# The output projection moved into the block of the mixers: last chunk's tail between dense products, samples' columns later

## The chip, the cores and the metric

One core of a Trainium2 chip. The metric is the device time of one execution in microseconds (us), smallest is best. The engines are TensorE (PE; PEld is its weight load), VectorE (DVE), ScalarE (ACT), GpSimd (POOL) and SyncE (SP, which issues most DMAs). They run side by side, each in its own program order, and wait for each other on semaphores.

## The reference, cut to what matters

One step of a hybrid decoder layer, for a prompt of 1024 tokens and 8 samples of 4 tokens (32 sample tokens; 1056 in all). Everything is float32.

```python
u = rmsnorm(x); q, k, v, z, xbc, dt = split(u @ w_in)
A = dilated_attention(q, k, v)              # prompt; samples attend to a cache of keys and values
y, ssm_state = ssd(conv(xbc), dt)           # Mamba-2 scan, chunks of 128 tokens
B = grouped_rmsnorm((y + d_skip * x) * silu(z))
h = x + concat(A, B) @ w_out                # the output projection: the stage of this change
y = h + relu(rmsnorm(h) @ w_up) ** 2 @ w_down
```

## The kernel before, in words

Features lie on the 128 partitions, tokens along the free axis. A dense product in float32 is three products of fp32r values: each operand is split into a high part (a cast) and a low part (the value minus the high part), and high by high, high by low and low by high are summed in PSUM. The 1056 token columns of a product are three groups of 352 columns (`GROUPS`, NG = 3), so one output tile costs, for each of KD = 8 input tiles, nine matmuls of 352 columns. The third group ends with the 32 sample columns.

The program has stages. `project` makes q, k, v. `weave` (in a block of its own, which stays open) makes the prompt's attention between the dense products of the remaining projections. `mixers` (line 1338) goes into the same block: eight rounds n = 0 to 7, each with chunk n of the prompt's scan and sample n's attention over the cache. `outward` (line 1987) holds the output projection, the samples' scan, and the feed-forward part. Before, `program.close()` in `build` (line 2661) ends the block between `mixers` and `outward`, and `outward` opens its own (line 2079).

**Start of the mixers.** SP loads the samples' q, keys, bias, then the rows of cumulated decays `ssd_m` (`load_rows(0)`, line 1421, 1 MB, behind a wait at line 1451 for a matmul twelve ticks before the end of `weave`), the chunk (`load_chunk`), the cache's values. GpSimd clears the diagonal query tile `sa_qdiag`, waits for the end of `weave`, clears the state, places sample 0's query (`place`, lines 1668 to 1678), clears two small tiles, prepares the samples' bias, and multiplies x by dt (`weigh_x`). TensorE does the scores of sample 0 (line 1497, behind `placed`), then turns x (`turn_x`, line 1552), `chunk_start`, and begins round 0 with `off(0, 0)` (line 1580). ScalarE makes the decays from the loaded rows (`segment`, lines 1753 and 1756) and then copies the turned x (`keep_x`, line 1764). VectorE starts with a wait for the stores of z (line 1935).

**Tail of the mixers.** After the last value products (lines 1520, 1524), TensorE turns y twice (`turn_y`, line 1560), gathers the sample's output (`sample_gather`, line 1542: 16 matmuls) and sums squares (`norm_sums`, line 1569). Between them VectorE has `keep_own` (1927), `keep_norm` of round 6 (1886, 1889), `add_skip` twice (1857), `gate` (1864), `keep_out` (1932), `keep_norm` of round 7; ScalarE `square` (1805); GpSimd `skipped` (1739) and `sum_squares` (1699, 1701).

**Start of outward.** The first half of w_out (tiles o = 0 to 7, which multiply A) is done in steps q = 8 o + k: `step(q)` (lines 2184 to 2201) is the nine matmuls of input tile k for output tile o, into the PSUM tile `wo_psa`. Input tile k of A comes from memory into one of three slots of `stage` (`load_a`), ScalarE casts it (`cast_a`, 2357), VectorE subtracts (`split_a`, 2445). Slots 0 to 2 and the first two weight tiles are loaded ahead, during round 5 (`ahead.load`, line 1479). A slot is loaded again after its `split_a`. The samples' scan stands in front of step 0 (transposes 2231 to 2236, sums 2241, decays 2244), behind step 3 (`ss_in`, 2253) and then between steps: `carried(b)` at the steps in OFF_AT, the first at q = 7, and `grown(b)` at those in STATE_AT. VectorE makes the masks for sample b in `own_rows(b)`. GpSimd splits the weights (2094, 2096): tile u needs slot u % 2 free (`w_used`).

```python
pe.wait_ge(w_split, o + 1); pe.wait_ge(a_lo_made, k + 1)     # step, o == 0
OFF_AT = {q: i // 2 for i, q in enumerate(PIECES) if i % 2 == 0}
for sem in retired: pool.sem_clear(sem)                       # outward's POOL, at u == 2
```

`kit.clear` and the loop at u == 2 set the semaphores of a finished stage back; `kit.prime` raises those of the feed-forward loops.

## Time and profile before

| | |
|---|---|
| time, median of 3 runs | 2105.92 us (2097.87 to 2106.04) |
| the profiled execution's own time | 2102.71 us |
| its span, first to last instruction | 2100.9 us |
| TensorE | busy 1996.1 us, 95% of the span |
| VectorE, ScalarE, GpSimd | busy 49%, 33%, 45% |
| mean granted TensorE clock | 0.987 of full speed |

The span starts at 0. The mixers take about 845 to 1101 us, outward begins at 1103.7 us. A line of a timeline gives start, length, engine, source line, operation, output and inputs, count, and in brackets how long the engine had been idle and what ended that. TensorE has two clock levels, 1.2 and 2.4 GHz; PEclk gives the granted one as a share of the higher, so 0.50 is the lower level and 1.00 the higher.

### The profile page before, as it was taken

Reading aid. Unit: us, or ns where it says so; the run is one execution under the profiler, and the core shown is the slowest. Engines: PE = TensorE matmul, PEld = TensorE weight load, DVE = VectorE, ACT = ScalarE, POOL = GpSimd, SP = SyncE. Lnnn points to the kernel's source line nnn. Section 1 sums busy time; section 2 is a strip of 40 time slices with the busy share of each in tenths; the row PEclk is TensorE's granted clock in tenths of the full one; section 3 lists DMA queues with packets and bytes.
Section 4 is the critical chain, followed back from the end, with each engine's and each line's share of the span. In section 5 each row is a group of like instructions: output and inputs, shape, how many; then the busy total and the mean of one; then the engine's idle time right before and its main releaser. Section 6 shows DMA issues by size and latency. Waiting matters only on the chain. (4 is left out here: it accounts for less than half of the span.)

```text
span 2100.9 us, 30132 instructions
## 1 busy us (share of the span) xinstructions
PE 1996.1 (95%) x11992; PEld 1816.7 (86%) x11992; DVE 1030.3 (49%) x1355; ACT 699.8 (33%) x1194; POOL 944.6 (45%) x580
## 2 busy tenths in 40 slices
PE   8999999888888999899989999999999999999999
PEld 7999998777777888565557789999999999999998
DVE  5888803877767665577767552522222212121212
ACT  5344323666666775555532021210010101010010
POOL 4688614777657665334423123243333334232332
PEclk9999999999999999899998999999999999999999
DMA  4354436444443443687845433111111111111112
GB/s 167 143 192 162 148 114 128 114 115 107 96 102 97 118 129 117 238 271 258 260 156 198 172 106 123 41 51 41 51 40 50 40 50 40 50 40 50 40 50 93
DMA packets 117926, 239.36 MB, mean 114 GB/s; under 512 B 29996, under 2 KB 63660, under 8 KB 116285
## 3 DMA queue, kind: packets, MB, share of 16 engines
q1 hardware_dynamic: 94956, 205.69, 31.2%
q10 hardware_dynamic: 22864, 32.25, 4.7%
q8 instruction: 69, 1.13, 0.2%
q14 instruction: 37, 0.30, 0.1%
HBM read 187.78 MB, written 58.67 MB: 117 GB/s over the span
## 5 line engine op out<-in xcount | busy, mean ns | idle before, releaser
L913 POOL TENSOR_SCALAR att_p<-att_p,att_rden 128x128 f32<-128x128 f32 (+7 forms) x128 | 250.6, 1965 | 132.9 <-DVE att_rden L1053 132.9
L2104 POOL CAST wo_hi<-wo_raw 128x1024 fp32r<-128x1024 f32 x64 | 66.7, 1042 | 492.6 <-issue 240.5
L2428 ACT ACTIVATE r_sq<-stage 128x1056 f32<-128x1056 f32 x32 | 34.8, 1088 | 624.5 <-DVE stage L2617 624.5
L2106 POOL TENSOR_TENSOR wo_lo<-wo_raw,wo_hi 128x1024 fp32r<-128x1024 f32 x64 | 187.3, 2926 | 5.1
L1058 DVE TENSOR_TENSOR att_pTlo<-att_t_ps,att_pThi 128x512 fp32r<-128x512 f32 x192 | 106.2, 553 | 109.0 <-ACT att_pThi L1173 107.6
L1173 ACT ACTIVATE att_pThi<-att_t_ps 128x512 fp32r<-128x512 f32 x192 | 93.3, 486 | 124.4 <-PE att_t_ps L995 117.3
L966 PE MATMUL dense_ps<-u_hi,w_hi 128*128 128x352 f32 x480 | 115.5, 342 | 16.3 <-DVE conv_pre L1085 7.8
L673 DVE RECIPROCAL proj_rinv<-proj_rinv 128x1056 f32<-128x1056 f32 x16 | 108.0, 6753 | 9.8 <-ACT proj_rinv L563 9.8
L2627 DVE TENSOR_TENSOR h<-h,wo_psa 128x1056 f32<-128x1056 f32 x32 | 40.2, 1255 | 144.2 <-PE wo_psa L2344 144.2
L1165 ACT ACTIVATE att_p<-att_p,att_min 128x128 f32<-128x128 f32 (+7 forms) x128 | 98.7, 772 | 32.7 <-DVE att_min L1071 31.7
L966 PE MATMUL dense_ps<-u_hi,w_lo 128*128 128x352 f32 x480 | 108.2, 334 | 0.0
L966 PE MATMUL dense_ps<-u_lo,w_hi 128*128 128x352 f32 x480 | 108.1, 333 | 0.0
L966 PEld LDWEIGHTS dense_ps<-u_hi,w_hi 128*128 128x128 f32 x480 | 81.3, 191 | 26.2 <-issue 17.4
L995 PE MATMUL att_t_ps<-const,att_p 128*128 128x128 f32 x576 | 95.6, 275 | 5.9 <-DVE att_pTlo L1058 2.0
L2627 DVE TENSOR_TENSOR h<-h,wo_psb 128x1056 f32<-128x1056 f32 x32 | 40.1, 1254 | 122.6 <-PE wo_psb L2344 122.6
L984 PE MATMUL att_s_ps<-att_k,att_qhi 128*128 128x512 f32 (+1 forms) x192 | 72.5, 382 | 28.5 <-DVE att_min L1071 23.7
L1071 DVE CUSTOM_DVE_ANT_0 att_p<-att_s_ps,att_bias 128x128 f32<-128x128 f32 (+7 forms) x128 | 93.5, 748 | 5.2 <-PE att_s_ps L985 5.2
L228 POOL TENSOR_TENSOR w_lo<-w_raw,w_hi 128x512 fp32r<-128x512 f32 (+1 forms) x52 | 91.7, 1764 | 5.4 <-POOL w_hi L226 0.2
L2094 POOL CAST wo_hi<-wo_raw 128x1024 fp32r<-128x1024 f32 x16 | 21.3, 1329 | 158.4 <-issue 110.0
L995 PEld LDWEIGHTS att_t_ps<-const,att_p 128*128 128x128 f32 x576 | 69.4, 141 | 23.9 <-issue 13.7
L1497 PE MATMUL sa_s<-sa_k,sa_qdiag 128*64 128x512 f32 (+1 forms) x256 | 78.3, 450 | 11.9 <-issue 11.9
L445 PE MATMUL proj_ps<-u_hi,w_hi 128*128 128x352 f32 x384 | 84.7, 329 | 4.4 <-POOL w_lo L241 4.4
(325 smaller groups left out, 5511.1 us busy)
## 6 DMA issues: line engine op xcount, KB each, us to landing
sa_k<-in_cache_k SPq DMA_DIRECT2D x32, 640.0 KB, 7.7
sa_v<-in_cache_v SPq DMA_DIRECT2D x40, 512.0 KB, 4.6
w_raw<-in_w_feat SPq DMA_DIRECT2D x36, 512.0 KB, 6.4
wo_raw<-in_w_up SPq DMA_DIRECT2D x32, 512.0 KB, 3.5
wo_raw<-in_w_down SPq DMA_DIRECT2D x32, 512.0 KB, 3.6
out_qk<-proj_out SPq DMA_DIRECT2D x16, 528.0 KB, 8.0
tmp_bias_rows<-tmp_table ACTq DMA_DIRECT2D x8, 1024.0 KB
att_bias<-tmp_bias_rows SPq DMA_DIRECT2D x16, 512.0 KB, 3.5
```

What stands on the lines that cost most here:

```text
L228: pool.tensor_tensor(self.lo[:, j, ks, :], raw, self.hi[:, j, ks, :].bitcast(F32), ALU.subtract).then_inc(self.split, 2 // parts)
L445: mm = pe.matmul(bank(acc[j], c, w), wt[:, j, k, :], xt[:, k, c:c + w], start=(k == 0 and wt is ring.hi and xt is x_hi), stop=(k == KD - 1 ...
L673: dve.reciprocal(rinv[:], rinv[:]).then_inc(inverted, 1)
L913: pool.tensor_scalar(slot(h, qt), slot(h, qt), rden[:, qt, :], None, ALU.mult).then_inc(normed, 1)
L966: mm = pe.matmul(bank(acc, c, w), wt[:, j, k, :], xt[:, k, c:c + w], start=(k == 0 and p == 0), stop=(k == KD - 1 and p == 2))
L995: mm = pe.transpose(t_ps[n % 2][:, c:c + P], slot(h, qt)[:, b * P:(b + 1) * P], kit.c(C_IDENT, P))
L1058: dve.tensor_tensor(p_lo[:, n % TURNED, off:512], t_ps[n % 2][:, off:512], p_hi[:, n % TURNED, off:512].bitcast(F32), ALU.subtract).then_i ...
L1071: dve.tensor_tensor_reduce(out=slot(h, qt), in0=s_ps[:, base:base + w], in1=bias[:, h % 2, SEQ - w:SEQ], scale=1.0, scalar=3e38, op0=ALU.a ...
L1165: act.activation(slot(h, qt), slot(h, qt), ACT.Exp, bias=low[:, qt, :], scale=-1.0, accum_out=den[:, qt, :]).then_inc(exped, 1)
L1173: act.activation(p_hi[:, n % TURNED, off:512], t_ps[n % 2][:, off:512], ACT.Copy).then_inc(hi_kept, 1)
L2106: pool.tensor_tensor(w_lo[:, j], raw_w, w_hi[:, j].bitcast(F32), ALU.subtract).then_inc(f_split[j], 1)
L2627: dve.tensor_tensor(grouped(h[:, o, :]), grouped(h[:, o, :]), in_banks(acc[j]), ALU.add).then_inc(f_added[j], 1)
```

## The change

`mixers` no longer ends with the tail of round 7: it hands the functions of its tail and its semaphores over in an object `Mixed`, and `outward` emits its engine programs into the same block, so that the block ends only after the last stage. Per engine:

- TensorE: for the first output tile, the eight steps first do only column groups 0 and 1 (six matmuls each), with the tail's `turn_y`, `turn_y`, `sample_gather` and `norm_sums` behind steps 0, 1, 2 and 4. Then come the samples' transposes, sums and decays, then the third column group of all eight steps, and `ss_in` behind step 7 instead of 3.
- ScalarE: casts of A's tiles 0 to 2, `square(7)`, casts 3, 4, the samples' cast, casts 5 to 7, and only then the copies of the samples' scan.
- VectorE: splits 0 to 4 between the tail's operations, then the samples' split, `steps`, splits 5 to 7, the rest.
- GpSimd: the first weight split before `skip_x(7)` and `sum_squares(7)`, the clears of semaphores at u == 8. At the start of the mixers: `place(0)` and the bias come before the wait for the end of `weave`; the clearing of the state waits in addition for all stores of z; `off(0, 0)` waits for all six of these (`zeroed`, 6).
- SP: `load_rows(0)` waits for the last value product of `weave`, `load_v(0)` for the last copies of its output; the samples' states are loaded between A's tiles 4 and 5, not first.
- Buffers: double tiles of the mixers are split in two, and `outward`'s buffers lie in an order that puts each over a tile that is dead by then; in PSUM `ssd_xturn` and `ssd_yturn` change places.

The diff, with changes of indentation alone left out (all of `outward` moves one level to the left), cut to its core:

```diff
@@ mixers, sync and tensor
-            sp.wait_ge(woven.flipped, TICKS * (NH - 1) + 1)
+            sp.wait_ge(woven.multiplied, TICKS * NH)
             load_rows(0)
             sp.wait_ge(woven.ring.made, woven.dense)
             sp.wait_ge(woven.feat_stored, woven.xbc_stores)
             load_chunk(0)
-            sp.wait_ge(woven.multiplied, TICKS * NH)
+            sp.wait_ge(woven.o_kept, 2 * NH)
             load_v(0)
...
-                    pe.wait_ge(zeroed, 1)
+                    pe.wait_ge(zeroed, 6)
...
-            turn_y(NC - 1, 0)
-            turn_y(NC - 1, 1)
-            sample_gather(NC - 1)
-            norm_sums(NC - 1)
+            mixed.pe_tail = turn_y, sample_gather, norm_sums
@@ mixers, gpsimd
             pool.memset(q_diag[:], 0.0).then_inc(zeroed, 1)
+            pool.wait_ge(q_loaded, 16 * (KB + 1))
+            pool.wait_ge(zeroed, 1)
+            place(0)
+            pool.wait_ge(common, 16)
...
+            new_bias(0)
             pool.wait_ge(woven.multiplied, TICKS * NH)
             pool.wait_ge(woven.ring.made, woven.dense)
             pool.wait_ge(woven.tail_stored, 16)
+            pool.wait_ge(woven.feat_stored, woven.stores)
             pool.memset(state[:], 0.0).then_inc(zeroed, 1)
-            place(0)
+            pool.wait_ge(zeroed, 4)
             pool.memset(new_stack[3 * NS:P, :].bitcast(F32), 0.0).then_inc(zeroed, 1)
             pool.memset(p_new[3 * NS:P, :].bitcast(F32), 0.0).then_inc(zeroed, 1)
...
-            new_bias(0)
             weigh_x(0)
@@ outward, gpsimd
+            skip_x, sum_squares = mixed.pool_tail
+            pool.wait_ge(mixed.k_used, mixed.scores)
             for u in range(2 * KD):
-                if u == 2:
-                    for sem in retired:
-                        pool.sem_clear(sem)
-                    kit.prime(pool)
+                if u == 1:
+                    skip_x(mixed.chunks - 1)
+                    sum_squares(mixed.chunks - 1)
...
+                if u == KD:
+                    for sem in retired:
+                        pool.sem_clear(sem)
+                    kit.prime(pool)
@@ outward, sync
-            load_state(0)
-            load_state(1)
-            load_state(2)
             for k in range(3, KD):
                 sp.wait_ge(a_lo_made, k - 2)
                 ahead.load_a(sp, dram, k)
+                if k == 4:
+                    sp.wait_ge(mixed.gated, mixed.chunks)
+                    sp.wait_ge(mixed.in_made, 2 * mixed.chunks)
+                    for b in range(3):
+                        load_state(b)
@@ outward, tensor
+            for k in range(KD):
+                pe.wait_ge(a_lo_made, k + 1)
+                step(k, (0, 1))
+                if k == 0:
+                    turn_y(last, 0)
+                if k == 1:
+                    turn_y(last, 1)
+                if k == 2:
+                    sample_gather(last)
+                if k == 4:
+                    norm_sums(last)
+            pe.wait_ge(mixed.y_skipped, 2 * mixed.chunks)
+            pe.wait_ge(mixed.o_kept, NB_DEC)
+            pe.wait_ge(mixed.norm_kept, mixed.chunks)
             pe.wait_ge(loaded, 48)
...
             for q in range(QS):
-                step(q)
-                if q == 3:
+                if q >= KD:
+                    step(q)
+                else:
+                    if q == 0:
+                        pe.wait_ge(as_made, 2)
+                    step(q, (2,))
+                if q == KD - 1:
                     pe.wait_ge(mix_made, 1)
@@ outward, scalar
             cast_a(0)
+            cast_a(1)
+            cast_a(2)
+            square(mixed.chunks - 1)
+            act.wait_ge(mixed.y_turned, 2 * mixed.chunks)
+            cast_a(3)
+            act.wait_ge(mixed.stored, 16)
+            cast_a(4)
+            act.wait_ge(mixed.o_kept, NB_DEC)
+            act.wait_ge(mixed.normed, mixed.chunks)
+            act.wait_ge(mixed.v_used, mixed.values)
             act.activation(m_hi[:, :, SEQ:NTOK], oT[:], ACT.Copy).then_inc(as_made, 1)
+            for k in range(5, KD):
+                cast_a(k)
             act.wait_ge(x_turned, 1)
@@ outward, vector
+            split_a(0)
+            keep_own(last)
+            add_skip(last, 0)
+            split_a(1)
+            add_skip(last, 1)
+            gate(last)
+            split_a(2)
+            keep_out(last)
+            keep_norm(last - 1)
+            split_a(3)
+            split_a(4)
+            keep_norm(last)
+            dve.wait_ge(as_made, 1)
+            dve.tensor_tensor(m_lo[:, :, SEQ:NTOK], oT[:], m_hi[:, :, SEQ:NTOK].bitcast(F32), ALU.subtract).then_inc(as_made, 1)
             dve.memset(off_sum[:], 0.0).then_inc(zeroed, 1)
...
+            for k in range(5, KD):
+                split_a(k)
             dve.wait_ge(kept, 2)
@@ build
-        program.close()
...
+        outward(kit, block, mixed, ahead, second, neg_a, skip, small[:, PAR_SSM:PAR_SSM + KD], small[:, PAR_FFN:PAR_FFN + KD], h, y_sums)
+        program.close()
```

## Rows read from the trace of the kernel before

**Rows 1.** Busy us (xinstructions) of PE, PEld, DVE, ACT, POOL; PEclk, DMA, GB/s, by stage.
```profile
858.87:884.00 25.13, 20.69 (x78) 14.42 (x77) 18.32 (x23) 9.60 (x17) 7.61 (x5) 0.66 0.75 249
...
915.16:944.37 29.21, 27.89 (x144) 17.25 (x142) 21.57 (x28) 16.61 (x36) 11.92 (x11) 1.00 0.78 260
...
1089.46:1131.62 42.16, 30.41 (x159) 24.33 (x156) 31.21 (x35) 16.42 (x19) 13.85 (x7) 0.72 0.40 133
1131.62:1260.00 128.38, 127.60 (x662) 102.81 (x662) 72.13 (x91) 11.63 (x18) 29.99 (x16) 1.00 0.44 151
1260.00:1320.00 60.00, 60.00 (x372) 59.75 (x372) 11.22 (x16) 5.86 (x6) 20.66 (x10) 1.00 0.34 117
```

**Rows 2.** TensorE in time around the block border: start, length (us), idle before.
```profile
1088.82 0.64 PE L1520 MATMUL sa_s<-sa_vhi,sa_pT 128*128 128x512 f32 x2
...
1093.60 1.09 PE L1560 MATMUL ssd_yturn<-const,ssd_y 128*128 128x128 f32 x4 [3.70 <-DVE h L1857]
1094.47 3.41 PE L1542 MATMUL sa_t<-const,sa_own 128*128 128x4 f32 x16
1099.95 1.22 PE L1569 MATMUL ssd_misc<-ssd_skip,const 128*128 128x128 f32 x4 [2.06 <-POOL ssd_skip L1701]
1103.72 1.86 PE L2231 MATMUL ss_in<-const,ss_xbc 128*32 128x128 f32 x8 [2.55 <-PEq L2661]
...
1116.53 1.25 PE L2196 MATMUL wo_psa<-mix_hi,wo_hi 128*128 128x352 f32 x3 [2.03 <-DVE mix_lo L2445]
...
1121.18 1.97 PE L2253 MATMUL ss_in<-ss_xdt,ss_m 32*32 32x64 f32 x32
```

**Rows 3.** VectorE there.
```profile
1091.15 1.75 DVE L1889 RECIPROCAL y_sums<-y_sums 128x256 f32<-128x256 f32 x1
...
1095.45 1.22 DVE L1864 TENSOR_TENSOR h<-h,ssd_z 128x1024 f32<-128x1024 f32 x1
...
1105.00 2.85 DVE L2504 TENSOR_TENSOR ss_steps<-const,ss_dta 32x512 f32<-32x512 f32 x1
1107.78 1.21 DVE L2445 TENSOR_TENSOR mix_lo<-stage,mix_hi 128x1024 fp32r<-128x1024 f32 x1
```

**Rows 4.** Columns as rows 1: one short stretch of the tail.
```profile
1095.00:1098.00 3.00, 2.89 (x14) 2.80 (x14) 1.71 (x3) 1.06 (x1) 0.16 (x1) 0.50 0.01 3
```

**Rows 5.** All engines, from the copy of the samples' inner product on.
```profile
1127.20 1.20 DVE L2529 COPY ss_y<-ss_in 32x1024 f32<-32x1024 f32 x1
...
1131.62 0.75 PE L2196 MATMUL wo_psa<-mix_hi,wo_hi 128*128 128x352 f32 x3
```

**Rows 6.** TensorE at the start of the mixers.
```profile
847.22 9.22 PE L1497 MATMUL sa_s<-sa_k,sa_qdiag 128*64 128x512 f32 x32 [2.14 <-issue]
...
858.87 1.02 PE L1580 MATMUL ssd_off<-ssd_state,ssd_xbc 128*128 128x512 f32 x2
...
863.46 1.54 PE L1590 MATMUL ssd_off<-ssd_xw,ssd_btok 128*128 128x512 f32 x2 [1.65 <-DVE ssd_y L1870]
```

**Rows 7.** ScalarE there.
```profile
849.28 1.28 ACT L1753 ACTIVATE ssd_m<-ssd_m,ssd_cum 128x128 f32<-128x128 f32 x4 [1.82 <-DVE silu_half L1118]
```

**Rows 8.** VectorE there.
```profile
858.51 0.85 DVE L1897 CUSTOM_DVE_ANT_0 sa_p<-sa_s,sa_bias 64x672 f32<-64x672 f32 x1 [10.04 <-DMA tmp_z<-silu_half]
```

**Rows 9.** GpSimd there.
```profile
845.13 0.95 POOL L1708 MEMSET ssd_state<- 128x1024 f32 x1 [19.83 <-PE att_pv_ps L1015]
...
847.17 0.95 POOL L1712 MEMSET sa_vnew<- 32x1024 f32 x1
```

**Rows 10.** DMA issues, 857 to 863: KB each, us to landing.
```profile
ssd_m<-tmp_cum_rows SPq DMA_DIRECT2D x1, 1024.0 KB, 6.5
...
ssd_z<-tmp_z SPq DMA_DIRECT2D x1, 512.0 KB, 4.4
```

**Rows 11.** GpSimd around the clearing of semaphores (L1743).
```profile
917.92 2.34 POOL L1739 TENSOR_TENSOR ssd_skip<-ssd_xbc,params 128x1024 f32<-128x1024 f32 x1
920.20 0.09 POOL L1684 MEMSET sa_bias<- 64x4 f32 x1
```

More of the change, by code:

```diff
@@ L1280 @@
     o_split: object
+    o_kept: object
     evicted: object
@@ L1973, in _, with outward @@
                     mix(n + 1, 0)
[L1974 removed]
                 if n + 1 < NC:
+                    keep_own(n)
                     mix(n + 1, 1)
                     scale_off(n + 1, 0)
[L1978 to L1987 removed]
+                    if n:
+                        keep_norm(n - 1)
+            mixed.dve_tail = keep_own, add_skip, gate, keep_out, keep_norm
+    return mixed
+def outward(kit, block, mixed, ahead, spent, neg_a, skip, gain, gain_ffn, h, y_sums):
     nc, dram = kit.nc, kit.dram
@@ new lines, in _ @@
+            pe.wait_ge(finish, 4)
+            pe.wait_ge(updated, NB_DEC)
+            products(0, (0, 1))
+            pe.wait_ge(ys_squared, 1)
+            for f in range(KD):
+                g = f // (KD // 2)
+                mm = pe.matmul(ys_ps[:, g * NS:(g + 1) * NS], kit.c(C_ONES, P), sq_s[:, f, :],
+                               start=(f % (KD // 2) == 0), stop=(f % (KD // 2) == KD // 2 - 1))
+            mm.then_inc(ys_summed, 1)
+            pe.wait_ge(half_evicted, 3 * KD)
+            products(1, (0, 1))
```

1093 lines of the change are left out of this document (543 added, 550 removed).

## The prediction

> **What bounds the kernel now.** I read the page first (its shares stand in the table above: TensorE busy 95% of the span), then the busy time by stage [rows 1]. The reader is to see where TensorE is not busy. In the feed-forward part it is busy 60.00 of 60 us with 372 matmuls, so a matmul of 352 columns costs 0.161 us at full clock; from step 8 of the output projection to 1260 us it is busy 127.6 of 128.4 us. Nothing there can take in a delay or a gain: what the border of the two stages wins or loses, the end wins or loses. The border is the stretch from the last value product (its end, 1089.46) to step 8 (1131.62): 42.2 us, TensorE busy 30.4, VectorE 31.2, mean clock 0.72. A last place is the start of the mixers, 858.9 to 884 us, with clock 0.66, which the change touches too; a steady round of the mixers has 29.2 us with TensorE busy 27.9.
>
> The third view is TensorE in time [rows 2]. The matmuls of the tail wait for VectorE (3.70 us) and GpSimd (2.06), then for the border of the blocks (2.55), then for `split_a` (2.03). The fourth is VectorE in time [rows 3], where the operations stand on which those matmuls wait. So this is a stretch bound by a relay between VectorE and TensorE, with 42.2 us for the work of some 23 us on TensorE at full clock (the terms of the walk below).
>
> **The change, part by part: the tail.** I walk from 1089.46 with the durations of the rows. Here the clock decides. A gap of 3.70 us in front of the second `turn_y` was enough that 95 to 98 ran at 0.50, the lower level of 1.2 GHz [rows 4], and the gather took 3.41 us there. The new tail has TensorE in bursts of 1.6 us with waits of 2 to 5 us between them, so I take the lower level from step 2 until step 7, at 0.3 us a matmul (the three of 1116.53 took 1.25 with their drain [rows 2]).
>
> 1. Step 0 with six matmuls 1.0 us (its weights and A's tile 0 are made beside the last value products, where VectorE waited in front of `keep_own` and GpSimd had nothing: no cost), `turn_y` 0.6, `add_skip` 0.7 (half of a `gate` and a bit), `split_a` 1.2, step 1 1.0, `turn_y` 0.6: 1094.6.
> 2. `add_skip` 0.7, `gate` 1.2, `split_a` 1.2 [rows 3]: 1097.7.
> 3. Step 2 at the lower level 1.8, gather 3.4 [rows 2]: 1102.9.
> 4. `keep_out` 0.2, `keep_norm(6)` 0.4 + 1.75, `split_a` 1.2: 1106.5. Steps 3 and 4 1.8 each, `norm_sums` 1.2: 1111.3.
> 5. `keep_norm(7)` 2.2, samples' split 0.4, clearing 0.9, `dta` 0.2, `steps` 0.6, splits 5 to 7 3.6: 1119.2. `steps` took 2.85 us beside a weight split of GpSimd [rows 3]. Here GpSimd has nothing to do at that time, so I take what 512 columns cost in `split_a`, half of 1.21. The loads of A's tiles 5 to 7 are issued from 1098 on, behind the three states, 3.4 to 8 us before they are cast: no cost; if that cover went, it would be one landing.
> 6. Rest of step 7 1.5; transposes, products and decays of the samples took 1103.72 to 1109.8 with 1.2 us of waiting, 4.9 us at the lower level; 3.7 here, half recovered: 1124.4.
> 7. The third group of eight steps, 24 x 0.161 = 3.9; `ss_in` 1.97 [rows 2]: 1130.2. Before, `ss_in` lay behind step 3, and its copy and the masks beside steps. Now VectorE's copy, `skipped`, `own_rows(0)` and then `carried(0)` stand in a row behind it: 1127.20 to 1131.62, 4.4 us [rows 5]: 1134.6.
>
> So step 8 comes at 1134.6 instead of 1131.6: **+3.0 us**. What the border removes (2.55 us of waiting, two DMA waits) is given back by the waits in items 3 to 7. If the clock stays up, items 3, 4 and 6 give back 2.3 + 2.0 + 1.7 = 6.0, and the tail is -3.0: the lower bound. For the upper, see the last rival.
>
> The Trainium skill, page "TensorE: Matmul & The Clock Gate", Part 4, says that transposes don't count as busy for the clock. By it the `turn_y` bursts do nothing to keep the clock, which would make it +3.0 rather than -3.0; no run so far separates that from the gaps.
>
> A second collision is in item 7. `w_used` for tile 0 now comes with the end of the third group, about 1128.3, and GpSimd then splits weight tile 2 for some 3.4 us, just when VectorE makes the masks with two inputs in SBUF. `steps` at 2.85 instead of 0.6 [rows 3] bounds that: 0 to 2.3 us. I take 0, since most of the chain is the copy out of PSUM. The page "SBUF — State Buffer", "SBUF: two separate sides", has an exclusive lock for such a pair of operations: by it the loser waits for the whole of the other's operation, and the sum would be 2 us higher.
>
> **The start of the mixers.** Sample 0's query is placed early, so the scores start at 845.1 instead of 847.22 and end at 854.3 [rows 6]. That alone wins nothing, for what follows waits for ScalarE, whose `segment` started at 849.28 [rows 7] and ended some 7.4 us later (four times 1.28 and an exponential), just as the scores did (856.4). Those now wait for `load_rows(0)`, issued at 845.1 instead of 14 us earlier. A megabyte of rows landed 6.5 us after its issue, half a us behind z, which landed in 4.4 [rows 10]: 2.6 us were its own, and 4.7 to 6.5 us from issue to landing are the bounds. The segments begin at 849.9 to 851.7: +0.6 to +2.4. Then `zeroed` 6: VectorE's first instruction shows that the last store of z landed at 858.5 [rows 8]; GpSimd's three memsets behind it cost 0.95 + 0.95 and about 0.1 for a small one [rows 9], so `off(0, 0)` can start at 860.6, against 858.87 [rows 6]: +1.7. With the stores later by the 2.6 us that the rows take on the same engines, it is +4.3; and with TensorE idle for 3 us in front of it, `chunk_start` and the two `off` are at the lower level, 1 us each. The next gate, `states(0, 0)` at 863.46, waits for `weigh_x(0)` behind the same memsets. I take **+2.5 us**, between +1 and +5. Rounds 1 to 7 repeat in 29.2 us and pass it on.
>
> **At no cost.** The clears of semaphores at u == 8 lie between tile 7's end and need, a whole tile of 72 matmuls = 11.6 us; those at line 1743 are not to be seen between 920.26 and 920.20 [rows 11]. `skip_x(7)` keeps its place (it waits for `norm_sums(6)`), behind the first weight split, done by 1084. The split tiles of the mixers change no access.
>
> **The sum.** The profiled execution took 2102.7 us; + 3.0 + 2.5 = 2108.2, so 2108. The median shown is 3.2 us above this execution and the lowest run 4.8 below it, so the runs scatter by as much as the change.
>
> **Rivals.**
>
> *Clock stays up.* Steps 0 to 4 lie closer than I think and the tail is -3.0; start +1 to +2.5: 2102. For: the steady rounds, 1.3 us idle in 29.2, stay at 1.00 [rows 1]. Against: the drop before 1095.
>
> *Faster by over 0.5%.* VectorE's own work in the tail is 31.2 us [rows 1], about 27 without the disputed `steps` and its like; if TensorE's bursts hid wholly beside it, step 8 would come at about 1119 (1089.5 + 27 + 2.2 for `carried(0)`), -12, and with the start at 0 it gives 2091. Against: the relays of items 1, 2, 3, 6 and 7 are written into the program order.
>
> *Slower, by the clock.* One mechanism: the half-speed tail does not recover before step 8, because third-group matmuls stand between transposes and small products. Place: 1094 to 1136. Price: step 1 and its `turn_y` 1.3, item 6 1.2, item 7's 24 matmuls 3.1 and `carried` 1.9, with the collision 2.3: 9.8 on top of +3.0 and +2.5: 2118. It decides when the third group's 24 matmuls take 7 us rather than 3.9. Against: the old kernel was at 1.00 again 3.2 us after step 0 began.
>
> *The change does not do what it says* (the added waits, for `y_summed`, `o_kept` or the retired tiles, hold the steps back until the old tail would have ended): the tail is +-0, the start +2.5, 2105. Against: each of the waits in front of steps 0 to 2 is for something that lies before 1089.
>
> **How the numbers follow.** A measurement of this kernel can tell about 0.5%, 10.5 us, from no change. Forecast 0.50, clock stays up 0.23, fourth rival 0.05, slower 0.13, faster 0.09. Faster by over 0.5% 0.09, slower 0.14 (with a small part of the forecast's upper end), within 0.77. The range reaches from the middle of the faster rival's way, 2095, to 2117.
>
> **What would show it.** Right: `ssd_m` landing at 850 to 852 and `off(0, 0)` at 860.6 to 863; `states(0, 0)` 1 to 5 us later than 863.46; rounds of 29.2 us; the gather near 3.4 us; step 8 44 to 46 us behind the last value product; then the same 128 us. Wrong: a gather of 1.9 us, step 8 less than 40 us behind, or a delay of the start over 5 us.

## The result, and the profile after

| | before | after |
|---|---|---|
| time, median of 22 runs each | 2105.16 us (2096.19 to 2110.53) | 2112.82 us (2103.45 to 2122.19) |
| ratio, 95% interval | | 1.0038 [1.0025, 1.0051] |
| the profiled execution's own time | 2102.71 us | 2109.35 us |
| its span | 2100.9 us | 2107.6 us |
| mean granted clock | 0.987 | 0.982 |

The change costs 8 us, with an interval of 5.3 to 10.7; the forecast was 2108 for the profiled execution, +5.5, and "within 0.5%". A second set of runs of the same kernel (a_again, below) gave 1.006 [1.0043, 1.0077]. So that the change is slower is clear; whether by less than 0.5% the two sets leave open.

Time by stage comes first, as in [rows 1], with stretches that end at the same events (last value product, step 8).

```profile
core 0: us, PE busy (x) PEld busy (x) DVE busy (x) ACT busy (x) POOL busy (x), PEclk, DMA share, GB/s
861.20:886.33 25.13, 19.84 (x85) 12.55 (x84) 17.80 (x23) 12.65 (x25) 9.30 (x7) 0.81 0.92 281
915.16:944.37 29.21, 27.87 (x143) 17.26 (x142) 21.55 (x29) 16.64 (x36) 11.92 (x11) 1.00 0.78 262
1088.61:1136.11 47.50, 30.62 (x159) 24.93 (x158) 25.41 (x34) 12.93 (x16) 10.07 (x7) 0.68 0.45 147
1136.11:1264.49 128.38, 127.60 (x661) 102.71 (x661) 76.79 (x91) 11.66 (x18) 26.65 (x14) 1.00 0.38 134
1330.00:1400.00 70.00, 67.73 (x405) 66.24 (x404) 34.07 (x20) 18.52 (x17) 22.07 (x10) 0.98 0.15 46
```

The steady round is the old one (29.21 us, TensorE busy 27.87), and so are the 128.38 us behind step 8. The border, from the last value product to step 8, is 47.50 us instead of 42.16 [rows 1]: +5.3. VectorE is busy 25.41 us in it instead of 31.21, so its work did get shorter; what got longer is the waiting: TensorE is idle for 16.9 us of the border instead of 11.8 (length less busy time), and its busy time is the same. From step 8 to the end of the span it is 971.5 us instead of 969.3, and the last line is where: the same stretch of the kernel before has clock 1.00.

TensorE in time, the counterpart of [rows 2] (start, length, and in brackets the idle time before and what ended it):

```profile
1088.46 0.88 PE L2223 MATMUL wo_psa<-mix_split,wo_hi 128*128 128x352 f32 x4
...
1092.01 1.22 PE L2223 MATMUL wo_psa<-mix_split,wo_hi 128*128 128x352 f32 x4 [1.92 <-DVE mix_split L2509]
...
1097.85 1.54 PE L2223 MATMUL wo_psa<-mix_split,wo_hi 128*128 128x352 f32 x4 [3.18 <-DVE mix_split L2509]
1099.78 3.41 PE L1557 MATMUL sa_t<-const,sa_own 128*128 128x4 f32 x16
1106.67 1.54 PE L2223 MATMUL wo_psa<-mix_split,wo_hi 128*128 128x352 f32 x4 [3.48 <-DVE mix_split L2509]
...
1109.98 0.60 PE L1584 MATMUL ssd_misc<-ssd_skip,const 128*128 128x128 f32 x4
1116.17 1.54 PE L2223 MATMUL wo_psa<-mix_split,wo_hi 128*128 128x352 f32 x4 [5.59 <-DVE mix_split L2509]
...
1123.30 0.59 PE L2223 MATMUL wo_psa<-mix_split,wo_hi 128*128 128x352 f32 x2
...
1127.34 1.97 PE L2303 MATMUL ss_in<-ss_xdt,ss_m 32*32 32x64 f32 x32
1132.03 0.61 PE L2237 MATMUL ss_misc<-ss_dta,ss_rown 32*128 32x16 f32 x2 [2.72 <-DVE ss_rown L2536]
1132.56 3.62 PE L2240 MATMUL ss_off<-ss_state,ss_cown 128*32 128x512 f32 x4
1136.11 1.06 PE L2223 MATMUL wo_psa<-mix_split,wo_hi 128*128 128x352 f32 x3
```

The block border's 2.55 us are gone. In their place stand five waits for VectorE, 1.92, 3.18, 3.48, 5.59 and 2.72 us: 16.9 us. The one stretch that answers to [rows 4], step 2 and the gather:

```profile
1098.00:1103.00 5.00, 5.00 (x22) 5.00 (x22) 0.00 (x0) 1.65 (x2) 4.84 (x4) 0.50 0.96 386
```

VectorE in time, the counterpart of [rows 3, 5]:

```profile
1095.44 1.23 DVE L1883 TENSOR_TENSOR h<-h,ssd_z 128x1024 f32<-128x1024 f32 x1
1096.58 1.22 DVE L2509 TENSOR_TENSOR mix_split<-stage,mix_split 128x1024 fp32r<-128x1024 f32 x1
1103.23 0.19 DVE L1951 COPY sa_oT<-sa_t 128x32 f32<-128x32 f32 x1 [5.43 <-PE sa_t L1557]
...
1114.30 0.68 DVE L2584 TENSOR_TENSOR ss_steps<-const,ss_dta 32x512 f32<-32x512 f32 x1
1114.91 3.47 DVE L2509 TENSOR_TENSOR mix_split<-stage,mix_split 128x1024 fp32r<-128x1024 f32 x3
...
1129.35 1.21 DVE L2603 COPY ss_y<-ss_in 32x1024 f32<-32x1024 f32 x1 [2.92 <-PE ss_in L2303]
1130.49 0.82 DVE L2604 TENSOR_TENSOR ss_skip<-ss_xbc,params 128x256 f32<-128x256 f32 x1
...
1131.70 0.27 DVE L2536 TENSOR_TENSOR ss_rown<-const 32x128 f32<-32x128 f32 x1
```

`steps` takes 0.68 us, as forecast, not 2.85 [rows 3]. The reader is to see two idle stretches: 5.43 us ahead of `keep_out`, which waits for the gather, while splits 3 and 4, for which TensorE will wait 3.48 us, stand behind it in VectorE's program; and 2.92 us ahead of the copy of the samples' inner product, while the masks for `carried(0)`, which need nothing of it, stand behind it.

The start of the mixers answers to [rows 6 to 10]. TensorE in time there:

```profile
845.10 9.26 PE L1512 MATMUL sa_s<-sa_k,sa_qdiag 128*64 128x512 f32 x32
855.86 0.63 PE L1567 MATMUL ssd_xturn<-const,ssd_xbc 128*128 128x128 f32 x4 [1.51 <-DMA ssd_xbc<-tmp_xbc]
859.00 1.12 PE L1567 MATMUL ssd_xturn<-const,ssd_xbc 128*128 128x128 f32 x4 [2.51 <-ACT ssd_xdt L1783]
...
861.20 1.92 PE L1595 MATMUL ssd_off<-ssd_state,ssd_xbc 128*128 128x512 f32 x2
...
865.98 1.13 PE L1605 MATMUL ssd_off<-ssd_xw,ssd_btok 128*128 128x512 f32 x2 [0.96 <-DVE ssd_y L1889]
```

ScalarE there (four segments of the decays, then the first copy of x):

```profile
850.87 1.28 ACT L1772 ACTIVATE ssd_m<-ssd_m,ssd_cum 128x128 f32<-128x128 f32 x4 [3.30 <-DMA ssd_m<-tmp_cum_rows]
...
858.35 0.60 ACT L1783 ACTIVATE ssd_xdt<-ssd_xturn 128x512 f32<-128x512 f32 x1
```

GpSimd there, its first two memsets:

```profile
856.07 0.95 POOL L1738 MEMSET ssd_state<- 128x1024 f32 x1 [17.53 <-DMA tmp_z<-silu_half]
857.08 0.95 POOL L1740 MEMSET sa_vnew<- 32x1024 f32 x1
```

VectorE there, its first instruction:

```profile
856.14 0.85 DVE L1916 CUSTOM_DVE_ANT_0 sa_p<-sa_s,sa_bias 64x672 f32<-64x672 f32 x1 [7.57 <-DMA tmp_z<-silu_half]
```

And the DMA issues from 840 to 870 us (KB each, us to landing):

```profile
ssd_m<-tmp_cum_rows SPq DMA_DIRECT2D x2, 1024.0 KB, 8.4
ssd_xbc<-tmp_xbc SPq DMA_DIRECT2D x2, 768.0 KB, 10.9
```

The segments start at 850.87, `off(0, 0)` at 861.20, `states(0, 0)` at 865.98 (before 863.46 [rows 6]). In this execution the last link of the chain is ScalarE's copy of x behind its four segments, not GpSimd: its three memsets were done at 858.1, three us before `off(0, 0)`. The stores of z landed at 856.1, earlier than before (858.5 [rows 8]). In four of the other executions with this start they landed as late as before, and the memsets came last; the section on the start below has them.

### The profile page after: what moved, and what is told of

Read it like the earlier page. It is cut to its first block, busy times and chain, and to the rows that moved or that the text cites. A ratio compares the mean times of both kernels' runs of the same rounds, so it can differ in the third digit from the quotient of the medians.

```text
span 2107.6 us, 30133 instructions
## 1 busy us (share of the span) xinstructions
PE 1998.3 (95%) x11992; PEld 1819.2 (86%) x11992; DVE 1026.3 (49%) x1355; ACT 700.2 (33%) x1194; POOL 938.7 (45%) x580
## 4 chain that ended last, share of the span: by engine, by line
PE 65%; DVE 7%; ACT 6%; issue 4%; POOL 1%; DMA 1%; ACTq 0%; DVEq 0%; SPq 0%; POOLq 0%
PE wo_psa L2376 9%; PE wo_psa L2394 9%; PE wo_psb L2376 9%; PE wo_psb L2394 7%; PE dense_ps L966 6%; PE wo_psa L2223 5%; PE sa_s L1512 3%; PE wo_psb L2328 2%; PE wo_psa L2328 2%; DVE att_p L1071 2%; PE att_t_ps L995 1%; ACT att_p L1165 1%; PE ssd_in L1616 1%; PE att_s_ps L984 1%; PE sa_s L1535 1%
## 5 line engine op out<-in xcount | busy, mean ns | idle before, releaser
L2132 POOL CAST wo_hi<-wo_raw 128x1024 fp32r<-128x1024 f32 x64 | 66.7, 1042 | 496.6 <-issue 242.3
L2492 ACT ACTIVATE r_sq<-stage 128x1056 f32<-128x1056 f32 x32 | 34.9, 1090 | 625.4 <-DVE stage L2691 625.4
L2376 PE MATMUL wo_psb<-mix_split,wo_hi 128*128 128x352 f32 x768 | 145.3, 324 | 0.0
L2376 PE MATMUL wo_psa<-mix_split,wo_hi 128*128 128x352 f32 x768 | 144.2, 322 | 0.0
L2376 PEld LDWEIGHTS wo_psb<-mix_split,wo_hi 128*128 128x128 f32 x768 | 128.6, 189 | 0.5 <-issue 0.5
L2376 PEld LDWEIGHTS wo_psa<-mix_split,wo_hi 128*128 128x128 f32 x768 | 128.0, 188 | 0.0
```

The lines of the kernel that those rows point to most:

```text
L2376: mm = pe.matmul(bank(acc[j], c, w), wt[:, j, k, :], xt[:, k, c:c + w], start=(k == 0 and wt is w_hi and xt is m_hi), stop=(k == KD - 1 an ...
```

## The experiments

Each median is of 12 executions (a_again and m_fill 6, t_all 5). Ratios are to the kernel before, timed beside the run, and are to be compared rather than medians, since the median of the kernel before itself was 2103.4 to 2106.6 us from one set of runs to the next. *Fillers* are matmuls that compute nothing used, put where TensorE waits. In the table, *mixers* is the time from the last product of `weave` to the last value product, *border* from there to step 8, *rest* from step 8 to the end of the span, each in the profiled execution.

| run | edit | median us | ratio [95%] | mixers | border | rest |
|---|---|---|---|---|---|---|
| before | | 2105.16 | 1 | 244.4 | 42.2 | 969.3 |
| after | | 2112.82 | 1.0038 [1.0025, 1.0051] | 243.4 | 47.5 | 971.5 |
| a_again | none | 2114.78 | 1.006 [1.0043, 1.0077] | 247.0 | 46.3 | 971.8 |
| s_alone | before + start | 2105.61 | 1.0004 [0.9994, 1.0015] | 247.8 | 42.0 | 969.3 |
| s_rows | before + late rows | 2105.43 | 1.0003 [0.999, 1.0016] | 242.4 | 41.7 | 970.9 |
| s_place | before + early place | 2104.88 | 1.0002 [0.9988, 1.0015] | 244.0 | 41.4 | 969.4 |
| m_fill | after + fillers, too long | 2115.91 | 1.0056 [1.004, 1.0071] | 247.4 | 46.2 | 971.5 |
| m_fit | after + fillers, fitted | 2106.88 | 1.0022 [1.0012, 1.0032] | 239.9 | 46.3 | 971.8 |
| t_masks | after, masks first | 2109.01 | 1.0021 [1.0006, 1.0037] | 248.0 | 41.5 | 969.7 |
| t_fill | after + fillers in the tail | 2106.67 | 1.0016 [1.0004, 1.0028] | 247.8 | 40.2 | 971.1 |
| t_order | after, splits first | 2107.95 | 1.0018 [1.0005, 1.003] | 247.4 | 39.4 | 971.7 |
| t_best | t_order + t_masks | 2099.94 | 0.9986 [0.9973, 0.9998] | 247.4 | 34.8 | 969.7 |
| t_all | t_best + fillers in start and tail | 2091.61 | 0.9943 [0.9928, 0.9957] | 244.9 | 31.2 | 971.3 |
| b_fill | before + fillers | 2099.86 | 0.9965 [0.9953, 0.9977] | 238.9 | 40.7 | 971.0 |

### Splitting the change: the start alone

s_alone puts the three edits of the start (rows, place, `zeroed` 6) into the kernel before.

> The kernel before with the start of the mixers alone changed (late rows, early placing, the clearing behind the stores of z, `zeroed` 6); the tail and the border of the blocks as before. Theory A (my prediction: the start costs +2.5 us): off(0, 0) at 861 to 862 instead of 858.9, round 1's off(1, 0) 1 to 4 us later than 885.4, ratio 1.001 to 1.002. Theory B (from the trace of after: the delay is taken in before round 1, since a wait for the clock of TensorE plays into it): off(0, 0) at 861 but off(1, 0) at 884.5 to 886, ratio 0.999 to 1.001, and the whole 8 us of the change lie in the tail. The border stays 42 us under both.

The end of `weave` is the end of its last value product: 845.07 us before, 844.63 here. Behind it `off(0, 0)` comes at 15.8 us instead of 13.8, the mixers are 3.4 us longer and the border is as before, 42.0. So the border's +5.3 belongs to the new tail. The borders of s_rows and s_place, 41.7 and 41.4, say the same. Round 1's `off(1, 0)` comes 43.8 us behind the end of `weave` instead of 40.4: theory A by the trace. The ratio, 1.0004, is the one of theory B, +0.8 us (-1.3 to +3.2): the 3.4 us of one profile are hardly above what the runs can tell.

### The start in two halves: s_rows and s_place

```diff
-            sp.wait_ge(woven.flipped, TICKS * (NH - 1) + 1)
+            sp.wait_ge(woven.multiplied, TICKS * NH)
             load_rows(0)
```

> The kernel before with only the load of the rows moved: it waits for the last product of the weave (and the values' load for the last kept outputs), as in the change; the query's place, the zeroing and the wait of the first state product stay as they were. Theory A (the late rows are what the start costs: they hold ScalarE's segments, and the chunk's own load lands beside them): segments begin at 850 to 851.5 instead of 849.3, the second turn_x waits 2 to 3 us for ScalarE, off(0, 0) at 860 to 861.5, and the last value product ends 2 to 4 us later behind the end of the weave; time +2 to +4 us (ratio 1.001 to 1.002). Theory B (my prediction's larger term: the wait for zeroed 6 behind the stores of z and the memsets): the rows alone cost under 0.6 us, off(0, 0) stays at 859 or earlier.

> The kernel before with only GpSimd's placing of sample 0's query and its bias moved ahead of the state's clearing; the state is cleared where it was and the first state product waits for that; the rows load is where it was. Scores begin about 2.1 us earlier. Theory A (ScalarE's segments, which begin at 849.3 as before, and their copy of x set the second turn_x): off(0, 0) is at most 1 us earlier than 858.9, the time moves by 0 to -1 us, ratio 0.9995 to 1.000. Theory B (the scores' end sets the rest of the start): all of the 2.1 us is won, ratio 0.999, and half of what the late rows cost is given back by this edit in the change.

The expectations give points in time (858.9) as in the profile of the kernel before. `weave` ends elsewhere in each execution, so here they are counted from its end. ScalarE's first segment comes at 4.2 us before the edit, at 5.5 with the late rows, at 4.2 with the early place; `off(0, 0)` at 13.8, 14.7 and 13.4. ScalarE in time in s_rows, its first segment:

```profile
854.07 1.28 ACT L1754 ACTIVATE ssd_m<-ssd_m,ssd_cum 128x128 f32<-128x128 f32 x4 [3.07 <-DMA ssd_m<-tmp_cum_rows]
```

And in s_place:

```profile
854.65 1.28 ACT L1754 ACTIVATE ssd_m<-ssd_m,ssd_cum 128x128 f32<-128x128 f32 x4 [1.78 <-DVE silu_half L1118]
```

The late rows cost 0.9 us and the early place gives 0.4. Theory A of s_rows holds for what waits for what, but not for its size: the last value product was to come 2 to 4 us later and came 2.0 us earlier (242.4 instead of 244.4). The reason is the clock again: from `states(0, 0)` to `states(1, 0)` it is 35.6 us, and 38.4 before, where TensorE's two inner products of round 0 took 3.5 and 3.7 us instead of 1.9 and 2.0. Of s_place, A. In the change `off(0, 0)` lies at 16.0 (s_alone 15.8), another 1.3 us later than with late rows alone. Most of that is the clock: from the second `turn_x` to `off(0, 0)`, the same ten matmuls, it takes 2.20 us in the change (859.00 to 861.20), 1.15 before (857.72 to 858.87), 1.16 in s_rows. With both edits TensorE idles for 1.5 and 2.5 us there and may fall to the lower level; it need not, for in a_again, with 1.4 and 2.4, it took 1.27 us and `off(0, 0)` lay at 14.9.

Which chain ends last also differs. The stores of z landed 10.9 us behind the end of `weave` in the change, and 10.7 to 12.7 in a_again, s_alone, m_fill, m_fit and t_fill, where `off(0, 0)` did not wait for GpSimd. In t_masks, t_order, t_best and t_all they landed at 13.2 to 13.7, as in the kernel before (13.4), and `off(0, 0)` waited for the last memset, 0.36 to 1.62 us. TensorE in time in t_order:

```profile
867.22 2.08 PE L1595 MATMUL ssd_off<-ssd_state,ssd_xbc 128*128 128x512 f32 x2 [1.22 <-POOL sa_pnew L1741]
```

Why the stores land at one time or the other no run shows.

### Fillers at the start: m_fill, m_fit

Matmuls of the identity, into a bank that nobody reads, where TensorE waits in round 0.

```diff
             turn_x(0, 0)
+            spin(24)
             turn_x(0, 1)
...
+                if n == 0:
+                    spin(6)
                 off(n, 1)
+                if n == 0:
+                    spin(6)
...
+                if n == 0:
+                    spin(16)
                 sample_values(n, 0)
```

> The changed kernel with matmuls of the identity into a free bank where TensorE waits in the first round of the mixers (24 ahead of the second turn_x, 6 ahead of off(0, 1) and of states(0, 0), 16 ahead of the first values): nothing of the program's own work changes. Theory A (the clock is part of the start's cost: 861 to 879 ran at the lower level in most executions): off and inner products of round 0 take 1.0 and 1.9 us instead of 2.0 and 3.5, the last value product ends 3 to 4.5 us earlier behind the scores' start (243.5 to 245 instead of 247.9), and the time is 2 to 4 us lower than the change's. Theory B (round 0 waits for VectorE and the loads, whatever TensorE's clock): under 1.5 us there, ratio as the change's, 1.003 to 1.004.

TensorE in time in m_fill, the first of them:

```profile
862.45 5.52 PE L1590 MATMUL ssd_yturn<-const 128*128 128x128 f32 x48
```

Each filler is two matmuls (48 for 24), so they took 5.5 us where 2.4 were free. The products of round 0 did run at full clock (1.02 and 1.89 us), but what the clock gave the filler took: nothing follows for the theories, only that a filler which is longer than the wait costs its excess.

> The changed kernel with fillers at the start again, now sized to the waits: 9, 2, 5 and 8 matmuls of the identity (0.23 us each at full clock, by the run before) instead of 24, 6, 6 and 16. Theory A (the clock is a part of the start's cost): round 0 at full clock up to the first values, last value product 243 to 245 us behind the scores' start instead of 247.4 to 248, time 3 to 4 us below the change's, ratio near 1.002. Theory B (round 0 is set by VectorE and the loads): 247 or more, ratio 1.0035 or more.

With 9, 2, 5 and 8 the mixers are 239.9 us, against 247.0 to 248.0 in the six profiles of the new start with round 0 at the lower level, and the ratio is 1.0022 against the change's 1.0038 and 1.006. Theory A, and by more than expected: the products of round 0 that took 2.0 and 3.5 us take 1.1 and 1.9. It is one profile, though: t_all below has the same fillers, its clock fell again within round 0, and its mixers are 244.9 us.

### The tail: t_masks, t_order, t_fill

t_masks: `skipped` and `own_rows(0)` ahead of the copy.

```diff
-            dve.wait_ge(in_made, 1)
-            dve.tensor_copy(y[:], in_ps[0:NS, :]).then_inc(in_kept, 1)
...
+            dve.wait_ge(in_made, 1)
+            dve.tensor_copy(y[:], in_ps[0:NS, :]).then_inc(in_kept, 1)
```

> The changed kernel with one edit: VectorE makes `skipped` and own_rows(0) before it waits for the samples' inner product, so that carried(0) does not stand behind the copy. Theory A (the serial chain product, copy, masks, carried costs 2.7 us of TensorE's idle time and, as a consequence, the lower clock in carried(0), 1.7 us): step 8 comes 4 to 5 us earlier, border 42.5 to 43.5 us instead of 47.5, ratio to before 1.001 to 1.002. Theory B (only the idle time counts, the lower clock comes anyway): 2.7 us earlier, carried(0)'s four matmuls still 3.6 us. Theory C (carried(0) waits for something else, such as the states' load): nothing moves.

Border 41.5, theory A, 1 us beyond its range. The end of it, TensorE in time:

```profile
1129.42 1.97 PE L2303 MATMUL ss_in<-ss_xdt,ss_m 32*32 32x64 f32 x32
1131.32 0.39 PE L2237 MATMUL ss_misc<-ss_dta,ss_rown 32*128 32x16 f32 x2
1131.64 1.90 PE L2240 MATMUL ss_off<-ss_state,ss_cown 128*32 128x512 f32 x4
1133.47 0.94 PE L2223 MATMUL wo_psa<-mix_split,wo_hi 128*128 128x352 f32 x3
```

From `ss_in` to step 8 it is 4.05 us (1129.42 to 1133.47) instead of 8.77 (1127.34 to 1136.11): 4.7 of the 6.0 saved come from here, 2.7 as the wait and 1.9 as `carried(0)` at full clock. The other 1.3 are the clock further up, and not the edit's doing: steps 1 and 2 run at full clock here, as they do in a_again, the change without an edit (border 46.3). Against that one the edit is worth 4.8.

t_order: VectorE's program in the order in which its inputs come (behind `gate`; left out are the clearing, `dta`, `steps` and the samples' split, which goes last). TensorE waits for `keep_norm` of round 6 ahead of `norm_sums`, since that now comes later.

```diff
             split_a(2)
-            keep_out(last)
-            keep_norm(last - 1)
             split_a(3)
             split_a(4)
-            keep_norm(last)
...
+            keep_norm(last - 1)
+            keep_out(last)
...
+            for k in range(5, KD):
+                split_a(k)
+            keep_norm(last)
...
-            for k in range(5, KD):
-                split_a(k)
```

> The changed kernel with VectorE's order in the tail changed: splits 3 and 4 and keep_norm(6) before keep_out, so they run beside the gather; the cleared sum and dta there too; splits 5 to 7 before keep_norm(7), `steps` and the samples' split. Theory A (VectorE idles 5.4 us for the gather and then makes TensorE wait 3.5 and 5.6 us by its order): the waits before steps 3 and 5 shrink to under 1 and 2.5 us, step 8 5 to 8 us earlier, border 40 to 42.5 us. Theory B (the tail is bound by the relay itself and by the clock): under 3 us earlier.

Border 39.4, theory A: step 3 no longer waits, step 5 waits 2.76 us instead of 5.59, a little more than the 2.5 expected, and the last wait is still 2.73 with the four products of `carried(0)` at 3.62 us. TensorE in time:

```profile
1118.56 1.46 PE L2223 MATMUL wo_psa<-mix_split,wo_hi 128*128 128x352 f32 x4 [2.76 <-DVE mix_split L2510]
```

t_fill: fillers ahead of steps 1, 2, 3 and 5 (8, 16, 18, 30 matmuls of 352 columns) and 14 ahead of `carried(0)`; VectorE's program untouched.

> The changed kernel with matmuls added that compute nothing used (8, 16, 18 and 30 of 352 columns before the waits of steps 1, 2, 3 and 5, and 14 before carried(0)), into PSUM that is dead there, so that TensorE is busy in the gaps. Theory A (the lower clock in the tail costs what the walk said, 2.3 in step 2 and the gather, 2.0 in steps 3, 4 and the sums, 1 to 2 behind them, 1.7 in carried(0)): gather 1.95 us instead of 3.41, step 8 6 to 8 us earlier, border 40 to 42 us, ratio about 1.000. Theory B (the gaps are VectorE's and ScalarE's time, and a faster TensorE waits longer): gather faster, but the border within 2 us of 47.5, ratio 1.003 to 1.005.

The border of t_fill, columns as in the first view:

```profile
1093.38:1133.60 40.22, 37.14 (x245) 32.01 (x245) 25.75 (x34) 13.04 (x16) 10.17 (x7) 1.00 0.47 159
```

Clock 1.00 throughout the border and 7.3 us less of it, with every real wait still there: TensorE waits another 0.3 to 0.8 us behind each filler, so none of them was too long. Theory A for the border; the ratio, 1.0016, stayed above the 1.000 expected. So 7.3 of the change's 47.5 us were the clock's (about 6 against the 46.2 to 46.3 of a_again, m_fill and m_fit), and t_order had 8.1 (6.9 against a_again) by order alone. The two overlap: a wait that is gone costs no clock either, as t_masks shows.

### Both repairs, and all together

> The changed kernel with both repairs of its tail: VectorE's order (the splits that the steps wait for ahead of the output copy, the norm and the samples' step) and the masks of the samples' chain ahead of the copy of its inner product. Theory A (the tail is a relay, and what the two repairs save adds as far as they shorten different waits): from the last value product to step 8 34 to 38 us instead of 47.5 and 39.4/41.5 with one of them; time 2101 to 2105, ratio to the kernel before 0.998 to 1.000. Theory B (both shorten the same stretch before step 8, or the time is moved by the clock elsewhere): border 39 to 41 us, ratio 1.001 to 1.002 as with either alone.

The border of t_best:

```profile
1098.10:1132.87 34.77, 26.92 (x158) 23.16 (x158) 25.30 (x34) 12.91 (x16) 11.99 (x7) 0.85 0.52 183
```

Border 34.8, theory A: counted from the 46.3 of a_again, whose first steps had the clock of t_order and t_masks, 46.3 - 6.9 - 4.8 would be 34.6, so the two add. This is a repair of the change without any padding, and it beats the kernel before, if barely: 0.9986 with an upper bound of 0.9998.

> Everything that helped together: the changed kernel with both repairs of its tail, the fitted fillers in round 0, and fillers ahead of steps 1, 2 and 5 (8, 16 and 14 matmuls of 352 columns, for waits of 1.9, 3.2 and 2.8 us). Theory A (the clock's part is still there to be won behind the repairs): border 29 to 33 us instead of 34.8, round 0 3 to 4 us shorter, time 2092 to 2098, ratio 0.994 to 0.997. Theory B (with the repairs VectorE sets the tail and the clock is worth little): border 34 to 36, ratio as with the repairs alone, 0.9985.

t_best, the fitted fillers of m_fit, and 8, 16 and 14 matmuls ahead of steps 1, 2 and 5. Its border:

```profile
1091.34:1122.51 31.17, 28.93 (x197) 24.28 (x197) 25.32 (x34) 13.05 (x16) 12.01 (x7) 1.00 0.59 204
```

0.9943, 12 us below the kernel before and some 21 below the change: theory A for border and time, but not for round 0, which was to be 3 to 4 us shorter. The mixers are 244.9 us, 2.5 less than in t_best, and 5.0 more than in m_fit with the same fillers. TensorE in time at the start, `off(0, 0)` and the second inner product of round 0:

```profile
862.26 1.13 PE L1599 MATMUL ssd_off<-ssd_state,ssd_xbc 128*128 128x512 f32 x2 [1.62 <-POOL sa_pnew L1752]
...
872.90 3.67 PE L1620 MATMUL ssd_in<-ssd_xdt,ssd_m 128*128 128x64 f32 x16
```

`off(0, 0)` waits for the last of GpSimd's memsets here, the gate that my forecast took for the binding one. The product of 3.67 us took 2.00 in m_fit: the fillers did not hold the clock up to it.

> The kernel before with fillers where its TensorE waits: 2, 2, 5 and 8 matmuls of the identity in round 0 of the mixers, 14 ahead of the last turn_y (a wait of 3.7 us), 7 ahead of the last norm_sums (2.06), and 11 matmuls of 352 columns ahead of step 2 (2.03); the border of the blocks (2.55) can't be filled. It asks whether the change is needed for what the whole set won (ratio 0.9943), or whether the old order with its clock held up does as well. Theory A (the new order with its repairs wins by itself, since steps lie in VectorE's gaps): the old order keeps VectorE's chain of 31 us, border 37 to 40 us instead of 42.2 (gather 1.8 instead of 3.4, block-start products at full clock at best), round 0 2 to 4 us shorter, time 2097 to 2101, ratio 0.997 to 0.9985. Theory B (the clock is all): border 33 or less, ratio 0.994 to 0.9955.

b_fill, the old order with fillers, comes to 0.9965. It lies nearer to theory A, just outside it on both sides: the border, 40.7, at a mean clock of 0.83, is above the 37 to 40 expected, and the mixers are 5.5 us shorter, more than the 2 to 4 expected. So some 60% of what t_all won needs no change at all. What the new order with its repairs adds is a border of 31.2 instead of 40.7; in the two profiles the new start and round 0 take 6.0 us of that back. The further 0.2% of t_all are hardly clear of noise: its interval ends at 0.9957, and that of b_fill begins at 0.9953.

### The change once more

> The changed kernel once more, without an edit, for a second profiled execution and more timed ones. Theory A (the clock in round 0 of the mixers and in the sums of the feed-forward part differs between executions of one kernel, and 863 to 873 us at full clock in the first profile of the change was the exception): here the last value product ends 247 to 248.5 us behind the scores' start instead of 243.5, the border is 45 to 48 us again, the time 2108 to 2114, ratio 1.002 to 1.005. Theory B (the first profile shows what the change does to the clock there): 243 to 244 again.

Theory A: 247.1 us from the scores' start, border 46.3, though the median, 2114.8, and the ratio, 1.006, lie just above the expected. In the first profile of the change round 0 ran at full clock in part (35.0 us from `states(0, 0)` to `states(1, 0)`), here and in the five other profiles of the new start without fillers there it did not (38.5 to 39.0). The tail differs too. TensorE in time here, step 1, step 2 and the gather:

```profile
1098.79 0.91 PE L2223 MATMUL wo_psa<-mix_split,wo_hi 128*128 128x352 f32 x4 [1.92 <-DVE mix_split L2509]
...
1103.64 0.92 PE L2223 MATMUL wo_psa<-mix_split,wo_hi 128*128 128x352 f32 x4 [3.18 <-DVE mix_split L2509]
...
1104.72 2.78 PE L1557 MATMUL sa_t<-const,sa_own 128*128 128x4 f32 x16
```

The waits are those of the first profile to the hundredth, but the lower level comes within the gather and not with step 1, and the border is 1.2 us shorter. In the four profiles in which the new tail stands as it is (after, a_again, m_fill, m_fit) the border is 47.5, 46.3, 46.2 and 46.3 us, +4.0 to +5.3: the profile shown first has the dearest.

## Why the prediction was right, point by point

**Sign and size.** Slower, inside 0.5%: right by the first set of runs; +5.5 forecast, +8.0 measured (5.3 to 10.7). The second set, 1.006, has +12.6 and lies outside 0.5%.

**Where the profiled execution stood.** It took 6.6 us more than the profiled one before, and I forecast 5.5 as +3.0 in the tail and +2.5 at the start. It came as +5.3 in the tail, -1.0 in the mixers and +2.2 in the feed-forward part. So the nearness of the sum is in part luck: `states(0, 0)` was 2.4 us later, as forecast, but 3.4 us came back in round 0 from a clock that the kernel before did not have there in its profile, and two terms that I did not have made up for it. In a_again the parts are +3.3 before the end of `weave`, +2.6, +4.1 and +2.5.

**The tail, items 1 to 7.** Counted from the last value product: step 2 forecast at +8.2, came at +9.2; the gather's end at +13.4, came at +14.6; `norm_sums`'s end at +21.8, came at +22.0; the third group at +34.9, came at +34.7; the end of `ss_in` at +40.7, came at +40.7 (1129.31). Up to there the walk held in this execution, and so did its premise: the gather took 3.41 us, and the stretch around it ran at 0.50. In a_again step 2 still ran at full clock and the gather took 2.78. Inside it two errors cancelled: the lower level began with step 1, not with step 2 (+1.0 there), and it ended within step 4, so that `norm_sums` took 0.60 us, and again ahead of the samples' products, which took 2.5 us (1120.78 to 1123.30) instead of 3.7.

**The term that failed** is the last of item 7, "4.4 us" from the end of `ss_in` to step 8. It was 6.8. The copy, `skipped` and the masks took 2.68 (2.27 before) and `carried(0)` 4.08 instead of 2.15. So of the missing 2.4 us 0.4 are VectorE's and 1.9 TensorE's at half clock. I took both from the old rows, where TensorE was at work until 0.19 us before; in the new order it idles for 2.72 us there and falls to the lower level. My rival *Slower, by the clock* had this term ("`carried` 1.9"), but only as part of a tail that never recovers. t_masks took the wait away and `carried(0)` took 1.90 again. With 1.9 + 0.4 the sum for the tail is the measured +5.3. My sign of being right, "step 8 44 to 46 us behind the last value product", was missed in the profiled execution (47.5); in a_again, m_fill and m_fit, with the same tail, it is 46.2 to 46.3, just above.

**The collision** of GpSimd's weight split with the masks was rated at 0 to 2.3 us and taken as 0. `skipped` took 0.82 us beside GpSimd's split and 0.41 in t_best, where it lay clear of it: 0.4 us. GpSimd in time, in the kernel before and in the change:

```profile
1104.91 2.40 POOL L2096 TENSOR_TENSOR wo_lo<-wo_raw,wo_hi 128x1024 fp32r<-128x1024 f32 x1
```

```profile
1128.69 2.34 POOL L2124 TENSOR_TENSOR wo_lo<-wo_raw,wo_hi 128x1024 fp32r<-128x1024 f32 x1
```

In the change VectorE came to `skipped` at 1130.49, 0.54 us before the split ended (1131.03); most of the split ran beside VectorE's wait and its copy out of PSUM. In the kernel before `steps` began at 1105.00, 0.09 us behind the start of the split, and ended 0.54 us behind its end; clear of a split it took 0.68. By the rule of the Trainium skill that I cited there (page "SBUF — State Buffer", "SBUF: two separate sides") whichever of the two operations starts first has the ports for its whole length, and the other is blocked. Both traces agree with it within 0.2 us. What was wrong is my price from it, 2 us: the price is what is left of the other's operation.

**The start.** +2.5 forecast for `off(0, 0)` and what follows; in the profiled execution `off(0, 0)` was +2.2 behind the end of `weave`, and in the six executions with round 0 at the lower level the mixers were 2.6 to 3.6 us longer than in the kernel before. The bounds for the landing of the rows (segments at 849.9 to 851.7) held: 850.87. What I had wrong for this execution is which chain ends last. I summed the stores of z (858.5) and three memsets (2.0) to 860.6; z landed at 856.1, the memsets were done at 858.1, and ScalarE's segments and copy came last, followed by TensorE at half speed (1.05 us more for the turn and `chunk_start`). That 861.20 lies by 860.6 is then luck of the path. In four of the ten profiles with this start the chain was the one I named. That z would land later by the 2.6 us of the rows no profile shows: it landed 10.7 to 13.7 us behind the end of `weave`, and 13.4 before.

**The rest**, "then the same 128 us": right (128.38). What I had no term for is 2.2 us after that, at the sums of the feed-forward part (clock 0.98 in 1330 to 1400 against 1.00). It comes and goes: of the profiles with the old tail three of five are at 1.00, of those with the new tail two of nine. Whether the change makes it likelier is open; no run was made on it.

**The rivals.** "Clock stays up" expected the border at 39.2 (-3.0); t_fill, which holds the clock up by force, gives 40.2, so its price was right to 1 us and its condition was not met. "Slower, by the clock" was to be decided by the third group's 24 matmuls, 7 us or 3.9: they took 4.0 (1123.30 to 1127.34), so it fell, though two of its prices came nearly true, step 1 with its `turn_y` (1.0 for 1.3) and `carried` (1.9). "Change does not do what it says" fell: steps 0 to 2 stand where the walk had them. "Faster, step 8 at 1119" had its price from VectorE's busy time alone; t_all, with all relays loosened, comes to 1122.5 - 1091.3 = 31.2 us where that rival had 29.2 (27 + 2.2). The change by itself did not come near it.

**On the clock and transposes.** By the Trainium skill ("TensorE: Matmul & The Clock Gate", Part 4) transposes don't keep the clock up. No run here isolates them: with the same waits of 1.92 and 3.18 us beside the same transposes TensorE was at the lower level from step 1 on in the change, and at full clock up to step 2 in a_again and t_masks.

## What to carry to other kernels

When dense products are laid between the operations of a relay, walk the in-order engine that feeds both: each operation that waits on the relay (here `keep_out`, the copy of `ss_in`) holds up the splits queued behind it. Two moves of lines in VectorE's program were worth about 11 us (0.9986 against 1.0038), more than the whole change lost. Then price each remaining wait twice: for itself, and for what the next small products cost at half clock; if a wait can't be removed, matmuls into a free bank, sized a little below it, can win back the second part.

## What the runs showed that I had not expected

TensorE's clock differs between executions of the same code, at places far from any edit. Windows 400 to 700, within `weave`, for t_masks and then b_fill, whose code there is the same:

```profile
400.00:700.00 300.00, 261.30 (x1549) 227.23 (x1548) 221.25 (x449) 190.69 (x369) 207.52 (x138) 0.98 0.42 105
```

```profile
400.00:700.00 300.00, 263.70 (x1515) 229.67 (x1514) 215.14 (x435) 188.10 (x362) 201.28 (x133) 0.95 0.41 105
```

The window of b_fill shows 34 matmuls fewer. The end of `weave` lay between 844.0 and 852.6 us (845.2 and 848.4 in the two profiles of the change itself), and the times of runs carry that scatter, so one profile's total says less than its stretches. Waits of the same length also end differently: behind 1.92 us of waiting step 1's first four matmuls took 1.22 us in the change and 0.91 in a_again, the same kernel.

Half clock is not only a price on what is late. In b_fill and m_fit a few us of matmuls that compute nothing, placed in waits of 0.8 to 2.5 us, went with mixers that are 5 to 8 us shorter (238.9 against 244.4; 239.9 against 247 to 248). With the fillers of m_fit in t_all it was 2.5 us, since the clock fell all the same.
